# Value rows laid as stripes for two token tiles, and one shared pass over the whole value table for the other two

## The chip, the cores and the metric

The kernel runs on one core of one Trainium2 chip. The metric is the device time of one execution in microseconds (us); of several runs the median is given. All arithmetic is in float32. The engines are TensorE (PE; PEld is its weight load), VectorE (DVE), ScalarE (ACT), GpSimd (POOL, which here issues the indirect gathers) and SyncE (SP, which issues the plain transfers).

## What is computed

One transformer block on 512 tokens of width 1024. Attention (8 "forgetting" heads, 4 differential heads) comes first, then a retrieval layer (PEER): each token has 8 query heads, each head picks its 16 best of 128 x 128 = 16384 experts, and an expert is one row of `u_tab` and one row of `v_tab` (1024 float32, 4 KB each).

```python
q = (xb @ w_q).reshape(PEER_TOKEN_BLOCK, PEER_HEADS, 2, PEER_HALF_DIM)
sc = jnp.einsum('thpd,hpkd->thpk', q, sub_keys).astype(jnp.float32)
s1, i1 = lax.top_k(sc[:, :, 0], PEER_TOPK)
s2, i2 = lax.top_k(sc[:, :, 1], PEER_TOPK)
cand = (s1[..., :, None] + s2[..., None, :]).reshape(PEER_TOKEN_BLOCK, PEER_HEADS, -1)
...
top_s, pos = lax.top_k(cand, PEER_TOPK)
eidx = jnp.take_along_axis(cidx, pos, axis=-1)
g = jax.nn.softmax(top_s, axis=-1).astype(xb.dtype)
u_sel = jnp.take(u_tab, eidx, axis=0)
hid = jax.nn.gelu(jnp.einsum('thkd,td->thk', u_sel, xb), approximate=False) * g
v_sel = jnp.take(v_tab, eidx, axis=0)
return jnp.einsum('thk,thkd->td', hid, v_sel)
```

So each token has 128 picks (8 heads x 16), and each pick wants a dot product with a u row and a weighted addition of a v row. The block ends with an RMS norm.

## The kernel before

**Tiles and stages.** The 512 tokens are four tiles of 128, one token to a partition. Attention is done for tile 0 first, then for tiles 1, 2 and 3 together (GROUPS). An order written by a planner (`ORDER`, lists of pieces such as `project`, `attend`, `outproj`, `query`, `keys`) is followed by PE, ACT and DVE alike. From the moment tile 0's first head has its scores, the retrieval layer of tile 0 is hosted in the same program: its steps are laid between the pieces of tiles 1 to 3 (`pieces_in`). Then a loop over tiles 1, 2, 3 does their retrieval alone.

**The search** (`topk_first`, `topk_second`) finds one head's 16 experts on DVE, lines 1123 to 1193. In the loop its first half follows one group of four dots and its second half the next.

**u rows.** POOL gathers one pick of all 128 tokens with one indirect transfer (L507, 128 rows of 4 KB = 512 KB) into a ring of four. DVE multiplies it with `hn` and sums (L1208, `dot`); ACT makes the gelu of four at once (L903); DVE multiplies with the gate (L1218).

**v rows.** POOL gathers them the same way (L515) into another ring of four, with u and v transfers by turns. For tile 0, DVE adds each row times its coefficient to `h` (L1228). For tiles 1 to 3, ACT makes a diagonal matrix of the coefficients (L910) and PE multiplies it with the row, in two halves of 512 columns, adding up in two PSUM banks (L730). A tile thus costs 256 gathers, 134 MB.

**Weights** of the projections come as 48 loads of 1 MB on SP's queue (L465) in pieces of 1 KB. PE turns the sub-keys over itself (`subkeys`).

## Time and profile before

| | |
|---|---|
| median of 2 runs | 1873.81 us (1871.68 to 1875.94) |
| span of the profiled execution | 1856.5 us |
| PE, DVE, POOL busy | 72%, 65%, 62% of the span |
| moved by DMA | 594 MB, 320 GB/s over the span |
| of which indirect gathers | 537 MB in 1024 transfers |

The span runs from the first to the last instruction; the profiled execution's own time is thus 1856.5 us plus what lies around it. Busy shares are averages over stages with different limits, so the stretches are read one by one: 0 to 123 us (tile 0's attention up to its first search), 123 to 535 (until the last attention piece of tile 3), 535 to 687 (queries and keys of tiles 1 to 3, and the rest of tile 0's retrieval), and three stretches of 390 us, one for each tile of the loop. In a timeline row the columns are start, duration, engine, line, operation, out<-in, count, and in brackets the idle time before it and who ended it. One float32 matmul of the program shows as two records.

### The profile page before, as it was taken

The numbers are of one execution on the slowest core, as the hardware profiler recorded it, in microseconds if no ns is written. First come the engines' busy times: TensorE is split into PE (matmuls) and PEld (weight loads), VectorE is DVE, ScalarE is ACT, GpSimd is POOL, SyncE is SP. The second block draws the span as 40 slices with busy tenths as digits, with TensorE's granted clock in tenths as the row PEclk, the third lists the DMA queues.
The fourth block names the chain that finished last, engine by engine and source line by source line (L and its number), as shares of the span: only waits on it lengthen the run. The fifth ranks groups of instructions, "written<-read, shape, count | busy, mean of one in ns | idle before, by whom it ended". The sixth has DMA issues, their size and how long they took to land.

```text
span 1856.5 us, 16630 instructions
## 1 busy us (share of the span) xinstructions
PE 1343.4 (72%) x3547; PEld 631.9 (34%) x3547; DVE 1198.2 (65%) x2864; ACT 439.1 (24%) x1049; POOL 1145.1 (62%) x1034
## 2 busy tenths in 40 slices
PE   6976898985588857666666666766777677766776
PEld 5655465572245532222222222222222222222222
DVE  2237768888998766665665566565665666656564
ACT  2323123343332122122121122112121221212112
POOL 0005645663456647777777767777777677777774
PEclk9987987986698988999999999999999999999899
DMA  9449968996689969999999999999999999999997
GB/s 305 152 139 353 348 238 277 322 346 232 229 300 325 345 228 339 347 365 348 342 365 335 347 330 349 351 352 356 347 364 327 338 372 354 365 342 368 340 360 263
DMA packets 196531, 594.24 MB, mean 320 GB/s; under 512 B 18544, under 2 KB 59512, under 8 KB 196472
## 3 DMA queue, kind: packets, MB, share of 16 engines
q0 software_dynamic: 147456, 536.94, 79.0%
q1 hardware_dynamic: 49016, 56.67, 9.3%
q8 instruction: 19, 0.31, 0.1%
q14 instruction: 40, 0.33, 0.1%
HBM read 591.44 MB, written 2.10 MB: 320 GB/s over the span
## 4 chain that ended last, share of the span: by engine, by line
DMA 26%; issue 14%; PE 12%; DVE 10%; POOL 7%; ACT 1%; DVEq 0%; POOLq 0%
DMA v_ring<-in_peer_v_dram,eidx 15%; DMA u_ring<-in_peer_u_dram,eidx 11%; PE acc L730 6%; DVE u_ring L1208 4%; POOL u_ring L507 4%; PE mm L580 3%; POOL v_ring L515 3%; PE acc L580 1%; DVE onehot L1175 1%; DVE picked L1186 1%; DVE onehot L1182 0%; DVE top_p L1165 0%; DVE top_v L1155 0%; DVE top_v L1162 0%; DVE top_hl L1169 0%
## 5 line engine op out<-in xcount | busy, mean ns | idle before, releaser
L730 PE MATMUL acc<-v_ring,diag 128*128 128x512 f32 x1536 | 802.2, 650 | 366.4 <-DMA v_ring<-in_peer_v_dram,eidx 353.6
L1208 DVE CUSTOM_DVE_ANT_0 u_ring<-u_ring,hn 128x1024 f32<-128x1024 f32 x512 | 619.4, 1224 | 388.4 <-DMA u_ring<-in_peer_u_dram,eidx 386.8
L507 POOL DMA_INDIRECT u_ring<-in_peer_u_dram,eidx x512 | 565.8, 1105 | 471.1 <-DVE hid L1208 185.4
L515 POOL DMA_INDIRECT v_ring<-in_peer_v_dram,eidx x512 | 577.2, 1127 | 226.3 <-issue 118.2
L730 PEld LDWEIGHTS acc<-v_ring,diag 128*128 128x128 f32 x1536 | 278.5, 200 | 889.5 <-issue 790.1
L903 ACT ACTIVATE gel<-hid 128x4 f32<-128x4 f32 x128 | 26.2, 205 | 880.1 <-DVE hid L1208 879.9
L1228 DVE SCALAR_TENSOR_TENSOR h<-v_ring,coef,h 128x1024 f32<-128x1024 f32 x128 | 164.4, 1285 | 4.4 <-DMA v_ring<-in_peer_v_dram,eidx 1.0
L910 ACT ACTIVATE diag<-ident,coef 128x128 f32<-128x128 f32 x384 | 131.7, 393 | 91.8 <-PE acc L730 62.3
L580 PE MATMUL mm<-actT,w_ring 128*128 128x384 f32 x336 | 126.1, 534 | 15.9 <-DMA w_ring<-in_w_in_dram 6.3
L580 PEld LDWEIGHTS mm<-actT,w_ring 128*128 128x128 f32 x336 | 69.3, 211 | 67.7 <-issue 20.9
L572 PE MATMUL mm<-w_ring,actT 128*128 128x256 f32 x304 | 77.0, 412 | 1.9 <-issue 0.8
L572 PEld LDWEIGHTS mm<-w_ring,actT 128*128 128x128 f32 x304 | 62.4, 210 | 13.0 <-issue 1.8
L580 PE MATMUL acc<-actT,w_ring 128*128 128x384 f32 x176 | 62.6, 511 | 3.6 <-issue 3.6
L903 ACT ACT_TABLE_LOAD x49 | 62.9, 1283 | 0.9
L1218 DVE TENSOR_TENSOR coef<-gel,gate 128x4 f32<-128x4 f32 x128 | 20.6, 161 | 57.2 <-ACT gel L903 57.2
L887 ACT ACTIVATE s_maps<-s_maps,negmax 128x128 f32<-128x128 f32 (+3 forms) x64 | 35.7, 558 | 75.1 <-DVE negmax L1084 74.8
L707 PE MATMUL tr<-ident,s_maps 128*128 128x128 f32 x120 | 26.8, 329 | 36.0 <-ACT pT L895 35.3
L690 PE MATMUL sc<-store 64*128 64x384 f32 (+3 forms) x86 | 35.0, 531 | 18.0 <-DVE negmax L1084 16.1
L580 PEld LDWEIGHTS acc<-actT,w_ring 128*128 128x128 f32 x176 | 34.9, 202 | 28.6 <-issue 8.4
L1208 DVE DVE_READ_ACCUMULATOR2_ANT hid<- 128x1 f32 x512 | 42.0, 82 | 0.0
L640 PE MATMUL mm<-w_ring,store 128*128 128x512 f32 x80 | 41.4, 668 | 0.0
L719 PE MATMUL o<-v_all,pT 128*128 128x64 f32 (+1 forms) x240 | 39.0, 302 | 0.4 <-ACT pT L895 0.2
(192 smaller groups left out, 1055.2 us busy)
## 6 DMA issues: line engine op xcount, KB each, us to landing
w_ring<-in_w_in_dram SPq DMA_DIRECT2D x18, 1024.0 KB, 11.1
w_ring<-in_peer_w_q_dram SPq DMA_DIRECT2D x16, 1024.0 KB, 8.8
u_ring<-in_peer_u_dram,eidx POOLq DMA_INDIRECT x512, 6.1
v_ring<-in_peer_v_dram,eidx POOLq DMA_INDIRECT x512, 6.2
v_ring<-in_w_in_dram SPq DMA_DIRECT2D x6, 1024.0 KB, 12.3
w_ring<-in_w_out_dram SPq DMA_DIRECT2D x6, 1024.0 KB, 11.3
h<-in_x_dram SPq DMA_DIRECT2D x4, 512.0 KB, 6.5
v_ring<-in_w_out_dram SPq DMA_DIRECT2D x2, 1024.0 KB, 5.0
```

The costliest lines, as they stand in the source:

```text
L507: nc.gpsimd.indirect_dma_start(out=u_ring[:, c % U_RING, :], out_offset=None, in_=peer_u[0], in_offset=bass.IndirectOffsetOnAxis(ap=eidx[p ...
L515: nc.gpsimd.indirect_dma_start(out=v_ring[:, c % V_RING, :], out_offset=None, in_=peer_v[0], in_offset=bass.IndirectOffsetOnAxis(ap=eidx[p ...
L572: last = nc.tensor.matmul(bk[:, 0:SLAB], actT[:, c, j * P:(j + 1) * P], w[:, c, :], start=(c == 0), stop=(c == KC - 1))
L580: last = nc.tensor.matmul(bk[:, 0:n], w[:, c, q * P:(q + 1) * P], actT[:, c, 0:n], start=(c == 0), stop=(c == KC - 1))
L640: last = nc.tensor.matmul(bk[:, :], qT[:, KC // 2 * hf + c, j * P:(j + 1) * P], w[:, c, :], start=(c == 0), stop=(c == KC // 2 - 1))
L719: last = nc.tensor.matmul(o_b[:, col:col + w], pT[:, k % 2, q * P:(q + 1) * P], v_all[:, q, vcol:vcol + w], start=(q == 0), stop=(q == t))
L730: last = nc.tensor.matmul(acc[half][:, :], diag[:, c % COLS, :], v_ring[:, c % V_RING, half * BANK:(half + 1) * BANK], start=(starts and c ...
L887: nc.scalar.activation(s, s, ACT.Exp, scale=-1.0, bias=negmax[:, m:m + 1], accum_out=rowsum[:, m:m + 1]).then_inc(exp_done, 1)
L903: nc.scalar.activation(gel[:, par, g0:g0 + COLS], hid[:, par, g0:g0 + COLS], ACT.Gelu).then_inc(gelu_done, 1)
L910: nc.scalar.activation(diag[:, c, :], ident[:, :], ACT.Copy, scale=coef[:, par, g0 + c:g0 + c + 1]).then_inc(diag_done, 1)
L1208: nc.vector.tensor_tensor_reduce(out=u_ring[:, c % U_RING, :], in0=u_ring[:, c % U_RING, :], in1=hn[:, :], scale=1.0, scalar=0.0, op0=ALU. ...
L1228: nc.vector.scalar_tensor_tensor(out=ht, in0=v_ring[:, c % V_RING, :], scalar=coef[:, par, c:c + 1], in1=ht, op0=ALU.mult, op1=ALU.add).th ...
```

## The change

- **Gathers.** The two rings of four become one ring of five slots of 512 KB (`row_ring`, ROWS). POOL's order is: 128 u rows of tile 0, 128 v rows of tile 0, the 384 u rows of tiles 1 to 3, the 128 v rows of tile 3. There are 768 indirect transfers in place of 1024.
- **Stripes** (tiles 0 and 3). A v transfer now fetches all 128 picks of one token, one to a partition. The picks' numbers and coefficients are turned over on PE (`swap`), and PE multiplies the row block with a weight of 32 columns of which one holds the token's coefficients (`pads`, `fill_pad` on DVE, `stripes` on PE). Four tokens go to four groups of 32 PSUM partitions. A step `i` has four tokens, each with two products of 512 columns; the next step's pad waits until the last has been used.
- **Shared pass** (tiles 1 and 2). DVE makes one-hot matrices for four tokens at a time (`onehots`), ACT scales one of them (four copies of 128 columns), PE multiplies them (four products of 128 columns) and ACT keeps the 512 results as weights (`keep_weights`): 32 such groups for each tile, until `region_a` and `region_b` hold, for tile 1 and tile 2, the weight of each token for each of the 16384 experts. Then SP streams the value table once in 128 blocks of 512 KB, and PE multiplies each block with both tiles' weights, four products of 512 columns (`values`).
- **Search.** Two heads are searched by one run of instructions (`topk`), at double width where the data allow it.
- **Order.** Tile 0's v steps stand behind the last attention piece, among the queries of tiles 1 to 3. All of tile 1's dots stand behind tile 0's last stripe; tile 2's dots are woven with the 32 weight groups of tile 1; 32 of tile 3's dots with those of tile 2; the other 96 with the pass over the table; tile 3's stripes stand behind the pass and behind the closing norms of tiles 1 and 2.
- **Layouts.** The host lays out the slabs in pieces of 8 KB for a partition and the sub-keys already turned; PE's turns of them and of the first gain are gone. The slab ring has three places.

```diff
-U_RING = 4
-V_RING = 4
-            def gather_u(n, par, c):
-                if not (isinstance(n, int) and n == 0 and c < U_RING):
-                    pool.wait_ge(dot_done, TOPK * n + c + 1 - U_RING)
...
-            def gathers(n, par, last):
-                for c in range(TOPK):
-                    ahead = c + COLS
-                    if ahead < TOPK:
-                        gather_u(n, par, ahead)
-                    elif not last:
-                        if ahead == TOPK:
-                            numbers_of(n + 1)
-                        gather_u(n + 1, 1 - par, ahead - TOPK)
-                    gather_v(n, par, c)
+ROWS = 5
+V_SLOTS = 4
+TOKENS = 4
+COLS = 32
+STRIPES = 4
...
+    early += [(16.0 + 8.0 * s, ("dots", 0, s)) for s in range(QUARTERS)]
+    met = max(16.0 + 8.0 * QUARTERS, PACE * attended + 1)
+    early += [(met + 1, ("coef", 0)), (met + 2, ("swap", 0))]
+    early += [(met + 12 + 6.0 * i, ("stripes", 0, i)) for i in range(COLS)]
...
+    ORDER += [("coef", 1), ("spread", 1)]
+    for s in range(QUARTERS):
+        ORDER += [("dots", 2, s), ("weights", 1, s)]
+        if s in (2, 8):
+            ORDER += searches(2, (s + 10) // 6)
+        if s in (12, 16, 20, 24):
+            ORDER += searches(3, (s - 12) // 4)
+    ORDER += [("gexp", 3, PH // 2 - 1), ("weights_end", 1), ("coef", 2), ("spread", 2)]
+    for s in range(QUARTERS):
+        ORDER += [("weights", 2, s)] + ([("dots", 3, s // 4)] if s % 4 == 3 else [])
+    ORDER += [("weights_end", 2)]
+    done_dots, done_rows = QUARTERS // 4, 0
...
+    ORDER += [("drain", 1), ("scale", 1), ("drain", 2), ("scale", 2)]
+    ORDER += [("stripes", 3, i) for i in range(done_rows, COLS)] + [("drain", 3), ("scale", 3)]
...
+            def row_free(r):
+                if r < ROWS:
+                    return
+                which, t = ROW_RUNS[(r - ROWS) // P]
+                c = (r - ROWS) % P
+                if which == "u":
+                    pool.wait_ge(dot_done, P * t + c + 1)
+                else:
+                    pool.wait_ge(row_used, P * GATHERED.index(t) + c + 1)
+                pool.nop(nofuse=True)
+            gather_scores(0)
+            gather_values(0)
+            for t in range(1, TILES):
+                gather_scores(t)
+            gather_values(TILES - 1)
...
+            def stripes(t, i):
+                k = COLS * GATHERED.index(t) + i
+                pe.wait_ge(pad_done, k + 1)
+                for g in range(STRIPES):
+                    r = row_no("v", t, STRIPES * i + g)
+                    pe.wait_ge(row_in[r % ROWS], 16 * (r // ROWS + 1))
+                    for half in range(2):
+                        last = nc.tensor.matmul(acc[t][half][COLS * g:COLS * (g + 1), :],
+                                                pads[:, g, COLS - 1 - i:2 * COLS - 1 - i],
+                                                row_ring[:, r % ROWS, BANK * half:BANK * (half + 1)],
+                                                start=(i == 0), stop=(i == COLS - 1), skip_group_check=True)
+                    last.then_inc(row_used, 1)
+            def weights(t, g):
+                k = GROUPS_W * MIXED.index(t) + g
+                pe.wait_ge(onehot_done, k + 1)
+                pe.wait_ge(scaled, k + 1)
+                if k >= len(w_banks):
+                    pe.wait_ge(w_copied, k + 1 - len(w_banks))
+                for i in range(TOKENS):
+                    last = nc.tensor.matmul(w_banks[k % len(w_banks)][:, i * P:(i + 1) * P],
+                                            picks_c[:, k % 2, i, :], picks_a[:, k % 2, i, :], start=True, stop=True)
+                last.then_inc(w_full, 1)
+            def values(m):
+                if m == 0:
+                    pe.wait_ge(w_copied, len(MIXED) * GROUPS_W)
+                    pe.wait_ge(drained, 2)
+                pe.wait_ge(v_in[m % V_SLOTS], 16 * (m // V_SLOTS + 1))
+                for t in MIXED:
+                    for half in range(2):
+                        last = nc.tensor.matmul(acc[t][half][:, :], wts[t][:, m, :], v_slots[m % V_SLOTS][:, BANK * half:BANK * (half + 1)],
+                                                start=(m == 0), stop=(m == K1 - 1), skip_group_check=True)
+                last.then_inc(v_used, 1)
...
-            def add_row(n, par, c):
-                dve.wait_ge(v_in[c % V_RING], 16 * (TOPK // V_RING) * n + 16 * (c // V_RING + 1))
-                dve.wait_ge(coef_done, GRP * n + c // COLS + 1)
-                if n or c:
-                    dve.wait_ge(v_used, TOPK * n + c)
-                ht = h[:, n // PH, :]
-                nc.vector.scalar_tensor_tensor(out=ht, in0=v_ring[:, c % V_RING, :], scalar=coef[:, par, c:c + 1], in1=ht,
-                                               op0=ALU.mult, op1=ALU.add).then_inc(v_used, 1)
...
+                elif kind == "weights":
+                    t, g = p
+                    k = GROUPS_W * MIXED.index(t) + g
+                    act.wait_ge(onehot_done, k + 1)
+                    for i in range(TOKENS):
+                        one = picks_c[:, k % 2, i, :]
+                        at = 2 * P + TOKENS * g + i
+                        last = nc.scalar.activation(one, one, ACT.Copy, scale=tcols[:, at:at + 1])
+                    last.then_inc(scaled, 1)
+                    if g > 0:
+                        keep_weights(t, g - 1)
+            def keep_weights(t, g):
+                k = GROUPS_W * MIXED.index(t) + g
+                act.wait_ge(w_full, k + 1)
+                nc.scalar.activation(wts[t][:, :, g * TOKENS:(g + 1) * TOKENS],
+                                     w_banks[k % len(w_banks)][:, :].rearrange("p (t i) -> p i t", t=TOKENS),
+                                     ACT.Copy).then_inc(w_copied, 1)
+            def fill_pad(t, i):
+                k = COLS * GATHERED.index(t) + i
+                if k > 0:
+                    dve.wait_ge(row_used, STRIPES * k)
+                nc.vector.tensor_copy(pads[:, :, COLS - 1:COLS], tcols[:, i:P:COLS].unsqueeze(2)).then_inc(pad_done, 1)
+            def onehots(t, g):
+                k = GROUPS_W * MIXED.index(t) + g
+                if k >= 2:
+                    dve.wait_ge(w_full, k - 1)
+                lo = g * TOKENS
+                for kept, at in ((picks_a, lo), (picks_c, P + lo)):
+                    last = nc.vector.tensor_tensor(out=kept[:, k % 2, :, :], in0=iota_f[:, :].unsqueeze(1).broadcast_to([P, TOKENS, K1]),
+                                                   in1=tcols[:, at:at + TOKENS].unsqueeze(2).broadcast_to([P, TOKENS, K1]),
+                                                   op=ALU.is_equal)
+                last.then_inc(onehot_done, 1)
...
+            def load_values(m):
+                if m < 2:
+                    sp.wait_ge(mm_full, len(MM))
+                elif m < V_SLOTS:
+                    sp.wait_ge(w_full, len(MIXED) * GROUPS_W)
+                else:
+                    sp.wait_ge(v_used, m - V_SLOTS + 1)
+                sp.dma_start(v_slots[m % V_SLOTS], peer_v[0][m * P:(m + 1) * P, :]).then_inc(v_in[m % V_SLOTS], 16)
```

**Place 1: DVE, between the dots of a tile after tile 0.** L1208 (before) and L1235 (change) are the dot of one gathered u row. In the loop of before, four dots are followed by the first half of the search for one head:

```order
1125 L1208 ISA u_ring,hid<-u_ring,hn 128x1024
1126 L1208 ISA hid 128x1
1127 L1217 ISA
1128 L1218 TENSOR_TENSOR coef<-gel,gate 128x4
1129 L1123 ISA
1130 L1123 COPY tk_s<-store 128x256
1131 L1112 ISA
1132 L1127 MAX tk_v<-tk_s 128x8 x2
```

In the change, twelve to twenty-four dots stand in a row, and then the whole search for two heads (it goes on for 13 more rows):

```order
677 L1235 ISA row_ring,hid<-row_ring,hn 128x1024
678 L1235 ISA hid 128x1
679 L1171 MAX topk_mem<-region_b 128x8 x4
680 L1174 MATCH_REPLACE topk_mem<-topk_mem,region_b 128x128 x4
681 L1176 MAX_INDEX topk_mem<-topk_mem,region_b 128x8 x4
682 L1179 MAX topk_mem<-topk_mem 128x8 x4
683 L1182 MAX_INDEX topk_mem<-topk_mem 128x8 x4
684 L1183 TENSOR_TENSOR topk_mem<-topk_mem 128x512
685 L1187 CAST topk_mem<-topk_mem 128x64
686 L1191 MAX gate<-topk_mem 128x8 x2
```

The search has moved from small pieces between groups of four dots to one block in front of the next dots.

**Place 2: PE, the queries of tiles 1 to 3.** Before, L580 are the query products (384 columns for three tiles) and L665 the key scores, with nothing else between them:

```order
288 L580 MATMUL mm<-actT,w_ring 128x384 x16
289 L580 MATMUL acc<-actT,w_ring 128x384 x8
290 L665 MATMUL mm<-subkT,qyT 128x128 x4
291 L665 MATMUL acc<-subkT,qyT 128x128 x2
292 L580 MATMUL mm<-actT,w_ring 128x384 x16
293 L665 MATMUL acc<-subkT,qyT 128x128 x2
294 L665 MATMUL mm<-subkT,qyT 128x128 x4
295 L580 MATMUL acc<-actT,w_ring 128x384 x8
```

In the change, L590 and L673 are the same products, and L707 are the striped products of tile 0 (32 result columns of weight, 512 moving columns; eight are one step of four tokens):

```order
258 L590 MATMUL bank<-region_a 128x384 x8
259 L707 MATMUL bank<-row_ring,pads 32x512 x8
260 L590 MATMUL bank<-region_a 128x384 x8
261 L707 MATMUL bank<-row_ring,pads 32x512 x16
262 L590 MATMUL bank<-region_a 128x384 x8
263 L707 MATMUL bank<-row_ring,pads 32x512 x8
264 L673 MATMUL bank<-region_b,stream 128x128 x6
265 L590 MATMUL bank<-region_a 128x384 x8
266 L707 MATMUL bank<-row_ring,pads 32x512 x16
```

PE has taken over tile 0's v rows, which DVE added before, and they stand between the queries.

**Place 3: PE, the end of the program.** Before, the loop body ends with a product pair for each v row of the tile:

```order
462 L730 MATMUL acc<-v_ring,diag 128x512 x2
463 L728 REGISTER_ALU
464 L730 MATMUL acc<-v_ring,diag 128x512 x2
465 L728 REGISTER_ALU
466 L730 MATMUL acc<-v_ring,diag 128x512 x2
467 L749 REGISTER_ALU
468 L749 COMPARE_AND_BRANCH
```

In the change the last blocks of the value table (L731, with the weights of tile 1 in `region_a` and of tile 2 in `region_b`) are followed by all 256 striped products of tile 3:

```order
561 L731 MATMUL bank<-stream,region_b 128x512 x2
562 L731 MATMUL bank<-stream,region_a 128x512 x2
563 L731 MATMUL bank<-stream,region_b 128x512 x2
564 L731 MATMUL bank<-stream,region_a 128x512 x2
565 L731 MATMUL bank<-stream,region_b 128x512 x2
566 L707 MATMUL bank<-row_ring,pads 32x512 x256
567 L290 UNCONDITIONAL_BRANCH
```

The v rows of the last tile stand behind the whole pass, on PE and on DVE alike.

## Rows read from the trace of the kernel before

**Rows 1.** Stretches: start:end, length, busy us (records) by engine, PE clock, DMA, GB/s
```profile
core 0: us, PE busy (x) PEld busy (x) DVE busy (x) ACT busy (x) POOL busy (x), PEclk, DMA share, GB/s
0.00:123.00 123.00, 97.99 (x423) 73.05 (x423) 30.42 (x95) 35.10 (x102) 2.05 (x10) 0.93 0.61 197
123.00:535.00 412.00, 321.69 (x1180) 207.79 (x1180) 342.50 (x753) 134.88 (x284) 217.91 (x187) 0.83 0.82 288
535.00:687.00 152.00, 121.51 (x408) 72.55 (x408) 117.26 (x215) 36.34 (x78) 86.56 (x73) 0.90 0.88 319
687.00:1077.00 390.00, 256.29 (x500) 88.56 (x500) 235.63 (x601) 77.07 (x195) 285.38 (x256) 0.96 0.93 341
...
1467.00:1856.50 389.50, 274.00 (x519) 95.54 (x517) 236.18 (x602) 78.70 (x197) 270.99 (x252) 0.94 0.92 342
```

**Rows 2.** The page's chain that ended last, by engine
```profile
DMA 26%; issue 14%; PE 12%; DVE 10%; POOL 7%; ACT 1%; DVEq 0%; POOLq 0%
```

**Rows 3.** Groups by shape in the loop, 690 to 1856 us: count, busy, mean, idle before
```profile
L730 PE MATMUL acc<-v_ring,diag 128*128 128x512 f32 x1536 | 802.2, 650 | 366.4 <-DMA v_ring<-in_peer_v_dram,eidx 353.6 <-ACT diag L910 12.5
L1208 DVE CUSTOM_DVE_ANT_0 u_ring<-u_ring,hn 128x1024 f32<-128x1024 f32 x384 | 463.3, 1225 | 380.1 <-DMA u_ring<-in_peer_u_dram,eidx 379.4 <-DVE hn L1235 0.6
...
L1175 DVE TENSOR_TENSOR onehot<-top_hlf,iota_f 128x512 f32<-128x512 f32 x24 | 16.6, 692 | 2.5
```

**Rows 4.** Stretch 123 to 535 us, DVE's dots (L1208) alone
```profile
123.00:535.00 412.00, 112.89 (x184) 0.83 0.82 288
```

**Rows 5.** The same stretch, DVE's row additions (L1228) alone
```profile
123.00:535.00 412.00, 112.49 (x88) 0.83 0.82 288
```

**Rows 6.** Timeline of DVE, the first search of one head, first and last instruction
```profile
122.92 0.29 DVE L1123 COPY tk_s<-store 128x256 f32<-128x256 f32 x1 [12.66 <-ACT store L863]
...
131.84 0.15 DVE L1193 TENSOR_SCALAR gneg<-top_v 128x1 f32<-128x1 f32 x1
```

**Rows 7.** Timeline of DVE, dots that find their rows landed
```profile
1820.68 1.23 DVE L1208 CUSTOM_DVE_ANT_0 u_ring<-u_ring,hn 128x1024 f32<-128x1024 f32 x1
...
1821.83 1.22 DVE L1208 CUSTOM_DVE_ANT_0 u_ring<-u_ring,hn 128x1024 f32<-128x1024 f32 x1
```

**Rows 8.** Timeline of PE, dense products: 8 of 384 columns, then 4 of 512
```profile
206.63 5.32 PE L580 MATMUL acc<-actT,w_ring 128*128 128x384 f32 x16
...
548.29 3.60 PE L640 MATMUL acc<-w_ring,store 128*128 128x512 f32 x8
```

**Rows 9.** Timeline of PE, two score products on the two halves of its rows
```profile
50.46 0.37 PE L690 MATMUL sc<-store 64*128 64x128 f32 x1
50.47 0.37 PE L690 MATMUL acc<-store 64*128 64x128 f32 x1
```

**Rows 10.** Timeline of POOL and DVE, the first gathers and the first dot
```profile
132.86 1.09 POOL L507 DMA_INDIRECT u_ring<-in_peer_u_dram,eidx  x1 [130.05 <-DVE gsum L1200]
134.26 0.94 POOL L507 DMA_INDIRECT u_ring<-in_peer_u_dram,eidx  x1 [0.30 <-issue]
...
137.65 1.23 DVE L1208 CUSTOM_DVE_ANT_0 u_ring<-u_ring,hn 128x1024 f32<-128x1024 f32 x1 [4.69 <-DMA u_ring<-in_peer_u_dram,eidx]
```

**Rows 11.** The page's DMA issues: count, median us from issue to landing
```profile
u_ring<-in_peer_u_dram,eidx POOLq DMA_INDIRECT x512, 6.1
v_ring<-in_peer_v_dram,eidx POOLq DMA_INDIRECT x512, 6.2
```

**Rows 12.** Timeline of PE, one v row of the loop (two products)
```profile
1219.78 1.98 PE L730 MATMUL acc<-v_ring,diag 128*128 128x512 f32 x4 [1.30 <-DMA v_ring<-in_peer_v_dram,eidx]
```

**Rows 13.** Timeline of ACT, four scaled copies of 128 columns
```profile
1205.77 1.28 ACT L910 ACTIVATE diag<-ident,coef 128x128 f32<-128x128 f32 x4 [0.31 <-DVE coef L1218]
```

**Rows 14.** Groups by shape up to 660 us, ACT's copies of 512 columns from PSUM
```profile
L895 ACT ACTIVATE pT<-tr 128x512 f32<-128x512 f32 x12 | 7.0, 583 | 2.2 <-PE tr L707 2.1
```

**Rows 15.** Timeline of the last tile's closing norm and store
```profile
1848.90 1.29 DVE L1247 TENSOR_TENSOR fin<-acc,h 128x512 f32<-128x512 f32 x2 [8.62 <-PE acc L730]
...
1853.48 0.33 SPq L486 DMA_DIRECT2D out_dram<-fin  x1
```

936 lines of the change are left out of this document (457 added, 479 removed).

## The prediction

> **What bounds the kernel now.** I read the stretches first [rows 1]. In the loop a tile takes 390 us, DMA is busy 92 to 93% at 341 to 342 GB/s, and no engine is above 73%. The groups of the loop say the same from the other side: PE waits 354 of its 366 idle us for v rows, DVE 379 of 380 for u rows [rows 3], and DMA leads the chain [rows 2]. So the loop is bound by its gathers: 390 us for 256 rows, 1.52 us a row, and search, diagonals and products all lie beside them. Before the loop it is different. From 123 to 535 us DVE is busy 343 of 412 us and PE 322, at 288 GB/s [rows 1]: two engines that wait for each other at close quarters. The profiled span is 1856.5 us and the median 1873.8, so 17.3 us lie around the span; I add them at the end.
>
> The change takes 67 MB out of 594 (two tiles' 134 MB of v rows against one table of 67 MB). At the loop's rate that is some 195 us. The question is whether transfers stay the bound. The new order puts the work in a row instead of side by side, so I cost it stage by stage, by what ends last in each.
>
> **A, start to first search: 125 us** (123 before). The turns of the sub-keys are gone and slabs come in larger pieces (minus 8), but the first search now wants head 1's keys too (plus 10).
>
> **B, tile 0's dots beside attention, 123 to 535 before: 380 us.** DVE loses 88 row additions, 112 us [rows 5], and gains the 36 of 128 dots that it has not done by then (184 records are 92 dots [rows 4]; one dot takes 1.15 us, start to start [rows 7]), 41 us. Its seven searches (9.1 us each, from 122.92 to 131.99 [rows 6]) become four of a pair. I cost a pair at 15.5 us: twice 9.1 less the copy and the small steps that are done once for both (bounds 14 and 18). DVE falls to about 275 us, and no longer sets the stage; PE's 322 us stay, with their waits for ACT and DVE. Bounds 322 and 412. The dots and searches come in its first half, where DVE is still the busier one, so I stay near the upper: 380.
>
> **C, queries of tiles 1 to 3 with tile 0's stripes: 250 us.** The stretch 535 to 687 (152 us) had 121.5 us of PE work [rows 1]; with the last output products it is 132. New are 256 products of 512 columns. Four such take 3.60 us with the drain, 0.855 us each [rows 8]; a step of eight is 6.8 us one after another, 219 in all. But two products on different halves of the array start 0.01 us apart [rows 9], so I expect the four 32-column groups to run beside each other, near 1.7 us a step, 55 in all. PE then needs 187 us; serial it would be 351. The rows set the rest: one v row occupies its slot from issue to landing (6.1 us [rows 11]), for PE's 1.98 us [rows 12] and the 0.3 us until POOL moves [rows 10], 8.4 us; with five slots that is 1.68 us a row, 215 for 128. And PE is away for 5.3 us with each of 16 query products [rows 8] while the ring stands full, of which I count some 35 us as not hidden. 250, bounds 187 and 351. Before, all of this and more lay in 152 us since the rows had been spread over B.
>
> The Trainium skill (TensorE: Matmul & The Clock Gate, Part 3) says that matmuls of 32 columns whose outputs lie in different groups of 32 partitions run at the same time, and gives 2.38 times for three of them. By that the striped step would be about 2.9 us, an estimate from the page's factor and the 6.8 us; the row of two halves starting together agrees in kind. The sum would be the same, the serial rival would fall.
>
> **D, tile 1's dots alone: 282 us.** Nothing else runs. A u row's slot is taken 6.1 + 1.15 + 0.3 = 7.55 us, a fifth is 1.51 us, the same as the loop's 1.52: 128 rows are 192 us. Now the searches stand in the way: six pair searches (four of tile 1, two of tile 2) of 15.5 us, 93 us, in which only the five slots fill. That gives back 1.5 us each, minus 9; the first gather behind the first search adds 6. Before, the same searches were hidden under the gathers, since DVE had 380 us to spare. Bounds: 246 (dots at 1.15) and 300.
>
> **E, tile 2's dots with tile 1's weight groups: 288 us.** A quarter of four dots (4.6) plus two one-hots of 512 elements (0.65 to 0.69 each [rows 3]) is 5.9 us of DVE, as much as four rows need; 32 of them 189, six searches 93, the turn between tiles 6. ACT's part of a group is 1.28 us for four scaled copies [rows 13] and some 0.6 to 0.8 for the 512-column copy [rows 14], hidden here. Bounds 280 and 305.
>
> **F, tile 2's weight groups with 32 dots: 90 us.** ACT needs 2.1 us a group, 67; DVE 32 x 1.3 + 32 x 1.15 = 78 and hands over at each; with turn and last copies 90. Bounds 76 and 105.
>
> **G, the pass: 439 us.** 128 blocks of four products, 512 x 0.855 = 438. This is the dearest term. The dense rows show no way out: 8 products of 384 columns take 5.32 us and 4 of 512 take 3.60, each with a drain of some 0.18, the same 1.67 ns for a column [rows 8], with weight loads hidden. Table and 96 u rows are 117 MB, 270 GB/s, well under the loop's 341: the transfers wait for PE here. Bounds 437 and 445.
>
> **H, tile 3's stripes alone: 228 us.** DVE first closes tiles 1 and 2 (4.6 us from drain to store [rows 15], 5.5 with ACT's squares, twice 11), then 5 of 128 rows are there (2 us), 123 come at 1.68 us (207), then the last norm and store, 8. Bounds: 178 (rows at POOL's 1.24 us from issue to issue [rows 10]) and 264 (stripes serial, 7.4 us a step).
>
> **Sum.** 125 + 380 + 250 + 282 + 288 + 90 + 439 + 228 = 2082 us of span, 2099 with the 17.3. The loop's 1169 us become 1327 (D to H), and the part before it, 687, becomes 755. 67 MB fewer are moved, but 438 us of PE products, 93 + 93 us of searches and the last tile's 207 us of rows no longer lie beside one another. What loses the cover: in G the gathers of tile 3's v rows could have run (only five do), in D and H PE stands still, in D and E DVE's searches are bare.
>
> **Rivals.**
> - *Transfers stay the bound.* If POOL, SP and the engines ran ahead of each other far enough, what follows tile 0 would be bytes: 335 MB (five times 67) at 342 GB/s, 981 us, after 687: 1685 with the 17.3. For it speaks that this is how the loop works today. Against it: a ring of five slots cannot run ahead by more than 7.5 us, and the pass alone costs 438 us of PE for 117 MB. It decides if D to H come to less than 1130 us (0.04).
> - *Every stage at its floor*: 118 + 322 + 187 + 246 + 280 + 76 + 437 + 178 = 1844, 1861 with the rest: no change (0.02).
> - *Faster rows.* With few transfers in flight a gather may land sooner than 6.1 us; then POOL's 1.24 us sets the pace. C falls by 35, D by 30, H by 50: 1984 (0.08). For it: the first gather of all, issued at 132.86, is in use at 137.65, 4.8 us later [rows 10]. Against it: 512 KB in 1.24 us is 423 GB/s, and the stretches of [rows 1] show no more than 342. The Trainium skill (DMA: Bandwidth & Descriptors, on the SWDGE path) gives about 2.0 us plus bytes over 436 GB/s for such a transfer, 3.2 us for 512 KB as an estimate; the trace's 6.1 is nearly twice that, and by the page's figure H would be at POOL's pace.
> - *Stripes run one after another*: C 351, H 254, 2226 (0.12). For it: each token's two halves share a column group and stand in a row, and nothing in the trace shows column groups.
>
> **Numbers.** The forecast's case has 0.74, its own range is 2040 to 2160 (B, C and H by 30 each). The range for 8 in 10 reaches to the serial stripes and leaves out the faster rows and the two cases below: 1990 to 2226. About 2% is what a measurement of this kernel can tell from no change. Faster by over 2%: 0.04; within: 0.02; slower: 0.94.
>
> **What would show it.** PE busy near 440 us without a gap in the pass, DMA near 270 GB/s there; DVE in D busy all through with idle gaps only between dots, 15 to 16 us for a pair search with POOL waiting meanwhile; POOL's idle time ended by dots and by striped products; PE nearly idle in D and H; in H about 1.7 us a row; the four striped products of a step starting close together. I would be wrong if the pass took much under 430 us, if the rows' pace left 1.5 to 1.7 us, or if C hid the stripes under the queries altogether.

## The result and the profile after the change

The changed kernel takes 2248.3 us (median of two runs, 2247.4 to 2249.2) where the kernel before, measured beside it, takes 1873.8: a ratio on record of 1.196 [1.187, 1.204] (the two medians alone give 1.200). That is slower, as forecast, but 149 us above the forecast 2099 and 22 us outside the range. The profiled run took 2247.4 us for a span of 2245.5, so only 1.9 us lie around the span, not the 17.3 that I had added: by spans the sum was 2082 and missed 163 us.

The stretches of the changed kernel, at the borders of the forecast's stages A to H (columns as in [rows 1]; a border can be drawn 1 or 2 us to either side):

```profile
core 0: us, PE busy (x) PEld busy (x) DVE busy (x) ACT busy (x) POOL busy (x), PEclk, DMA share, GB/s
0.00:129.00 129.00, 102.70 (x428) 76.79 (x429) 29.38 (x93) 33.82 (x101) 2.15 (x10) 0.91 0.55 200
129.00:433.00 304.00, 202.27 (x718) 131.94 (x718) 234.08 (x551) 50.87 (x132) 159.85 (x128) 0.79 0.78 273
433.00:557.00 124.00, 106.27 (x432) 67.50 (x432) 48.30 (x138) 43.67 (x101) 0.00 (x0) 0.88 0.12 43
557.00:855.00 298.00, 264.05 (x934) 103.66 (x933) 14.34 (x45) 27.76 (x58) 120.52 (x128) 0.96 0.74 254
855.00:1153.00 298.00, 0.95 (x4) 0.50 (x3) 241.04 (x615) 5.05 (x22) 167.84 (x133) 0.51 0.67 232
1153.00:1461.00 308.00, 65.47 (x256) 56.98 (x256) 273.09 (x671) 63.43 (x191) 163.40 (x128) 0.50 0.66 220
1461.00:1562.00 101.00, 55.36 (x259) 50.55 (x259) 78.61 (x133) 56.05 (x161) 36.71 (x30) 0.67 0.46 151
1562.00:2004.00 442.00, 441.47 (x1026) 195.34 (x1026) 122.25 (x203) 4.99 (x9) 143.55 (x99) 1.00 0.72 270
2004.00:2245.50 241.50, 199.28 (x513) 44.40 (x512) 15.22 (x47) 6.17 (x16) 115.55 (x123) 0.96 0.79 274
```

| stage | forecast | measured | missed |
|---|---|---|---|
| A start | 125 | 129 | +4 |
| B tile 0's dots beside attention (two rows above) | 380 | 428 | +48 |
| C tile 0's stripes beside the queries | 250 | 298 | +48 |
| D tile 1's dots | 282 | 298 | +16 |
| E tile 2's dots, tile 1's weights | 288 | 308 | +20 |
| F tile 2's weights, 32 dots | 90 | 101 | +11 |
| G pass | 439 | 442 | +3 |
| H tile 3's stripes, closing | 228 | 241 | +13 |

Against [rows 1] one sees where the loop's overlap went. No stage moves 341 GB/s on average any more. PE is busy for 441 of the pass's 442 us at full clock, at 270 GB/s, as forecast. D has PE at nothing, H has DVE at next to nothing. The pass's average hides two halves, which the forecast had not told apart, with tile 3's dots beside it and without them:

```profile
1562.00:1762.00 200.00, 199.47 (x461) 88.34 (x462) 119.61 (x196) 3.55 (x8) 138.84 (x94) 0.99 1.02 402
1762.00:2004.00 242.00, 242.00 (x567) 107.00 (x565) 2.63 (x8) 1.44 (x2) 4.70 (x5) 1.00 0.48 160
```

The first moves 402 GB/s, more than any stage before the change, so 341 GB/s was not a ceiling for all transfers; the second moves 160, with POOL doing five gathers in 242 us. The chain of work that ended last is led by PE now, where DMA led it [rows 2], and the page's groups show the costs of a row:

```profile
PE 45%; DVE 22%; DMA 16%; issue 11%; POOL 4%; ACT 2%; POOLq 0%; DVEq 0%; ACTq 0%
...
L537 POOL DMA_INDIRECT row_ring<-in_peer_u_dram,eidx x512 | 666.6, 1302 | 664.8 <-DVE hid L1235 362.2
L1235 DVE CUSTOM_DVE_ANT_0 row_ring<-row_ring,hn 128x1024 f32<-128x1024 f32 x512 | 618.0, 1225 | 217.9 <-DMA row_ring<-in_peer_u_dram,eidx 215.0
L548 POOL DMA_INDIRECT row_ring<-in_peer_v_dram,row_t x256 | 240.8, 941 | 657.1 <-PE bank L707 410.5
L707 PE MATMUL bank<-row_ring,pads 128*32 128x512 f32 x1024 | 345.2, 628 | 66.8 <-DMA row_ring<-in_peer_v_dram,row_t 33.3
```

POOL stands 362 us for dots (L1235) and 410 us for striped products (L707): the five slots are what the gathers wait for. 200 of the 410 are one wait, from 1819 us to the first striped products of H: tile 3's first five v rows fill the ring, and nothing uses them before the pass is over. And a u row's gather takes POOL 1302 ns where a v row's takes 941, with the same instruction.

### The profile page after: what moved, and what is told of

Its sections match the earlier page's. It is cut to its first block, busy times and chain, and to the rows that moved or that the text cites. A ratio compares the mean times of both kernels' runs of the same rounds, so it can differ in the third digit from the quotient of the medians.

```text
span 2245.5 us, 14698 instructions
## 1 busy us (share of the span) xinstructions
PE 1437.8 (64%) x4564; PEld 727.7 (32%) x4564; DVE 1056.3 (47%) x2494; ACT 291.8 (13%) x788; POOL 909.6 (41%) x778
## 4 chain that ended last, share of the span: by engine, by line
PE 45%; DVE 22%; DMA 16%; issue 11%; POOL 4%; ACT 2%; POOLq 0%; DVEq 0%; ACTq 0%
PE bank L731 20%; DMA row_ring<-in_peer_u_dram,eidx 10%; PE bank L707 9%; DVE row_ring L1235 7%; DMA row_ring<-in_peer_v_dram,row_t 6%; PE bank L590 4%; PE bank L582 4%; POOL row_ring L537 4%; PE bank L647 3%; DVE stream L1283 2%; PE bank L720 2%; PE bank L785 1%; DVE topk_mem L1209 1%; DVE topk_mem L1214 1%; DVE topk_mem L1217 1%
## 5 line engine op out<-in xcount | busy, mean ns | idle before, releaser
L537 POOL DMA_INDIRECT row_ring<-in_peer_u_dram,eidx x512 | 666.6, 1302 | 664.8 <-DVE hid L1235 362.2
L1235 DVE CUSTOM_DVE_ANT_0 row_ring<-row_ring,hn 128x1024 f32<-128x1024 f32 x512 | 618.0, 1225 | 217.9 <-DMA row_ring<-in_peer_u_dram,eidx 215.0
L548 POOL DMA_INDIRECT row_ring<-in_peer_v_dram,row_t x256 | 240.8, 941 | 657.1 <-PE bank L707 410.5
L707 PE MATMUL bank<-row_ring,pads 128*32 128x512 f32 x1024 | 345.2, 628 | 66.8 <-DMA row_ring<-in_peer_v_dram,row_t 33.3
L720 PE MATMUL bank<-stream 128*128 128x128 f32 x512 | 120.0, 416 | 285.5 <-issue 235.7
L731 PE MATMUL bank<-stream,region_a 128*128 128x512 f32 x512 | 242.5, 596 | 0.7 <-ACT region_b L973 0.7
L731 PE MATMUL bank<-stream,region_b 128*128 128x512 f32 x512 | 240.6, 592 | 0.0
L707 PEld LDWEIGHTS bank<-row_ring,pads 128*32 128x32 f32 x1024 | 78.7, 112 | 322.0 <-issue 138.6
L590 PE MATMUL bank<-region_a 128*128 128x384 f32 x512 | 180.7, 511 | 1.5 <-issue 0.8
L582 PE MATMUL bank<-region_a 128*128 128x256 f32 x512 | 129.7, 413 | 14.6 <-DVE stream L1033 13.0
L731 PEld LDWEIGHTS bank<-stream,region_a 128*128 128x128 f32 x512 | 97.6, 191 | 123.0 <-issue 122.0
L731 PEld LDWEIGHTS bank<-stream,region_b 128*128 128x128 f32 x512 | 97.5, 190 | 123.0 <-issue 123.0
L590 PEld LDWEIGHTS bank<-region_a 128*128 128x128 f32 x512 | 100.3, 200 | 78.8 <-issue 20.5
L582 PEld LDWEIGHTS bank<-region_a 128*128 128x128 f32 x512 | 105.0, 210 | 32.7 <-issue 15.7
## 6 DMA issues: line engine op xcount, KB each, us to landing
region_b<-in_keys_t_dram SPq DMA_DIRECT2D x1, 1024.0 KB, 12.6
```

Source lines behind the costliest of these rows:

```text
L537: nc.gpsimd.indirect_dma_start(out=row_ring[:, r % ROWS, :], out_offset=None, in_=peer_u[0], in_offset=bass.IndirectOffsetOnAxis(ap=eidx[: ...
L548: nc.gpsimd.indirect_dma_start(out=row_ring[:, r % ROWS, :], out_offset=None, in_=peer_v[0], in_offset=bass.IndirectOffsetOnAxis(ap=row_t[ ...
L582: last = nc.tensor.matmul(bk[:, 0:SLAB], actT[:, c, j * P:(j + 1) * P], w[:, c, :], start=(c == 0), stop=(c == KC - 1))
L590: last = nc.tensor.matmul(bk[:, 0:n], w[:, c, q * P:(q + 1) * P], actT[:, c, 0:n], start=(c == 0), stop=(c == KC - 1))
L707: last = nc.tensor.matmul(acc[t][half][COLS * g:COLS * (g + 1), :], pads[:, g, COLS - 1 - i:2 * COLS - 1 - i], row_ring[:, r % ROWS, BANK ...
L720: last = nc.tensor.matmul(w_banks[k % len(w_banks)][:, i * P:(i + 1) * P], picks_c[:, k % 2, i, :], picks_a[:, k % 2, i, :], start=True, s ...
```

## The experiments

All are edits of the changed kernel. The kernel before, measured again beside each group of them, came out at medians of 1853 to 1879 us, up to 1.4% apart; so sizes below are read from stretches of the traces, and medians only where they differ by more. The changed kernel itself was not measured again beside them. rows4, bareB, nostripes0, onehalf and thin6 are single runs. The tables give lengths in us.

### The ring's depth: rows4, rows6

`ROWS = 5` becomes 4 and 6 (for room, rows6 gives the value table three slots and loads one of its blocks early, not two).

> The changed kernel with a ring of four rows instead of five. Theory 'a slot's time sets the pace': in the changed kernel a u row comes every 1.61 us in the stretch of tile 1's dots and a v row every 1.75 us in tile 3's stripes, five slots, so a slot is taken 8.05 and 8.75 us; with four it is 2.0 and 2.2 us a row: tile 1's dots 298 -> about 345 us, the last stretch (tile 3's stripes and closing) 241 -> about 295, tile 0's stripes 298 -> about 345, in all about 2420 to 2450. Rival 'POOL's issue sets the pace of u rows (1.26 us of gather and 0.3 between), PE's serial products (4 x 0.43 us) that of v rows': tile 1's dots stay near 300 unless four slots take over at 6.1+1.15+0.3 = 7.55 us, 1.89 a row (+25 us at most), the last stretch stays within 15 us; in all under 2350.

> The changed kernel with a ring of six rows; for the room the value table's slots are three instead of four and only the first block is loaded early. Theory 'a slot's time sets the pace': 1.34 us for a u row, 1.46 for a v row, tile 1's dots 298 -> about 270, the last stretch 241 -> about 205, tile 0's stripes 298 -> about 270, in all about 2140 to 2160. Rival 'POOL's issue and PE's serial products set the pace': tile 1's dots 298 and the last stretch 241 unchanged, 2240 to 2255. The pass stays at 442 us in both (a block's slot is free for 3 x 3.45 us).

Measured: 2383.5 and 2169.2 us (ratio 1.167 [1.159, 1.174]).

| slots | B | C | D | H | 24 rows between two searches of D | v row in H |
|---|---|---|---|---|---|---|
| 4 | 454 | 324 | 330 | 274 | 44.9 | 2.06 |
| 5 | 428 | 298 | 298 | 241 | 38.5 | 1.81 |
| 6 | 408 | 280 | 289 | 217 | 38.0 | 1.63 |

(The v row's pace is first product to last in H, over the rows that come after the ring's first filling. C runs from the swap to the last striped product.) Each theory holds in a part. In C and H, where PE uses the rows, and in B, where DVE has attention to do beside them, the gain goes on with the sixth slot. In D it all but stops at five: 38.5 and 38.0 us for the same 24 rows. (The pass, expected to stay at 442 us, took 451 in rows6; the total is so much the higher.) And a slot's time isn't fixed as I had assumed: H's pace times the slots is 8.2, 9.1 and 9.8 us, so with more slots each is taken for longer.

### What slows a u row: thin6

rows6 with dots over 64 of the 1024 columns:

```
-                    nc.vector.tensor_tensor_reduce(out=row_ring[:, r % ROWS, :], in0=row_ring[:, r % ROWS, :], in1=hn[:, :],
+                    nc.vector.tensor_tensor_reduce(out=row_ring[:, r % ROWS, 0:64], in0=row_ring[:, r % ROWS, 0:64], in1=hn[:, 0:64],
```

> rows6 with dots over 64 of the 1024 columns (the rest of each dot is left out): DVE is nearly idle between rows, all rows are still gathered whole. Theory 'DVE at work slows POOL's gather issue from 0.94 to 1.3 us, which with 0.3 between sets 1.58 us a row': the issue falls to 0.94 us and a u row to 1.24 to 1.3 us in the stretch of tile 1's dots (24 rows between two searches in 30 to 31 us instead of 38). Rival 'the transfers set it': 1.5 to 1.6 us a row still.

POOL from the end of D's second search to the start of its third, in the changed kernel, in rows6, in thin6 and in rows4 (count, busy us, mean ns, idle before):

```profile
L537 POOL DMA_INDIRECT row_ring<-in_peer_u_dram,eidx x23 | 30.7, 1336 | 20.2 <-DVE hid L1235 13.5 <-issue 6.7
```
```profile
L537 POOL DMA_INDIRECT row_ring<-in_peer_u_dram,eidx x22 | 30.6, 1391 | 20.0 <-DVE hid L1235 13.5 <-issue 6.4
```
```profile
L537 POOL DMA_INDIRECT row_ring<-in_peer_u_dram,eidx x23 | 21.5, 937 | 20.1 <-DVE hid L1235 13.5 <-issue 6.6
```
```profile
L537 POOL DMA_INDIRECT row_ring<-in_peer_u_dram,eidx x23 | 30.8, 1340 | 26.6 <-DVE hid L1235 21.7 <-issue 4.9
```

In thin6 the issue falls to 937 ns, the 24 rows from 38.0 to 29.1 us, D by 40 us to about 249; the whole takes 2036.6 us. The 13.5 us of waiting for a dot are the search before the stretch. With five and six slots POOL waits for nothing more, so between searches it is POOL's own issue that paces u rows (1.3 to 1.4 us and 0.3 between); with four it waits 8 us more, and the slots count as well. The issue is long because DVE's dots run: behind pieces of searches in early's C, 79 gathers take 991 ns each. The Trainium skill names the sharing: the GPSIMD Engine Reference (Specifications, row on the SBUF interfaces) has GpSimd's access to SBUF contend with DVE instructions with two SBUF inputs, which the dots are; 937 against 1391 ns fits that. The row gives no size and does not speak of gathers.

### The searches: split, early

split cuts every search of D and E but the first in pieces, one behind each group of four dots:

```
-        if s in (2, 8, 14):
-            ORDER += searches(1, (s + 4) // 6)
...
+        if s >= 2:
+            ORDER += pieces(*((1, (s + 4) // 6) if s < 20 else (2, (s - 20) // 6)), (s - 2) % 6, 6)
```

> The changed kernel with each pair search from tile 1's second on cut in pieces of seven to eight steps, one behind each group of four dots, instead of 13.7 us at one stretch. Theory 'rows and searches stand one after another, as the ring holds five rows only': DVE's small gaps between dots (1.61 - 1.18 us a row) take the pieces in; tile 1's dots fall from 298 to about 245 us (DVE alone: 128 x 1.18 + 6 x 13.7 = 233), tile 2's from 308 to about 285 (DVE alone 273), in all about 2170 to 2190. Rival 'DVE and POOL slow each other, so that a row takes 1.6 us of gather issue whenever DVE works': each piece just makes the gathers late, the gain is under 30 us: 2220 to 2250.

Measured: 2178.1 us (1.175 [1.168, 1.183]); D 272, E 278. E fell 7 us below its forecast (DVE 271 of 278 us busy: it is DVE's stretch). D stayed 27 above its own. There the issue still takes 1262 ns, and POOL still waits 39 us for dots; the two were not told apart. early takes the pieces out of D and E instead, three behind each striped step of tile 0 from the thirteenth on:

```
+    for i, p in enumerate(tail):
+        ORDER.append(p)
+        if p[0] == "stripes":
...
+            take(3)
```

> The changed kernel with the searches of tiles 1 to 3 in six pieces each, three pieces behind each striped step of tile 0 from its thirteenth on, where DVE has nothing but pads; only six searches' worth of pieces less one stay in tile 1's dots. Theory 'D and E are long since 12 searches stand bare in them': both become 128 rows at 1.6 us, 205 to 225 us instead of 298 and 308; C stays near 298 (pieces of 7 us lie beside a step of 8.9 us), in all 2248 - 165 = about 2080. Rival 'pieces hold up the pads, and C grows by what D and E lose': 2180 or more.

```profile
546.00:852.00 306.00, 263.09 (x934) 102.00 (x934) 150.07 (x627) 33.65 (x98) 129.13 (x133) 0.98 0.75 255
852.00:1078.00 226.00, 0.87 (x3) 0.50 (x3) 184.67 (x381) 3.08 (x12) 155.57 (x128) 0.50 0.86 294
1078.00:1303.00 225.00, 66.35 (x259) 57.49 (x259) 194.63 (x329) 56.56 (x161) 148.51 (x128) 0.50 0.88 303
```

These are C, D and E of early. Ten of the twelve searches are in C now; the other two lie in pieces in D. DVE does 136 us more in C and C grows by 8; D and E lose 155, a little more than the ten searches' 138 us. The whole takes 2086.6 us (1.126 [1.119, 1.133]), forecast 2080. The prediction had called the searches of D and E bare, and they are, by their full size.

### Tile 0's dots beside attention: bareB, spreadB

bareB puts all of them behind the attention, spreadB a group of four every 13.6 shares instead of every 8:

```
-    early += [(16.0 + 8.0 * s, ("dots", 0, s)) for s in range(QUARTERS)]
+    early += [(16.0 + 13.6 * s, ("dots", 0, s)) for s in range(QUARTERS)]
```

> The changed kernel with all of tile 0's searches and dots moved behind the attention of tiles 1 to 3. It shows what the attention needs alone. Theory 'tile 0's dots and searches hold DVE, and with it attention, in the first 304 us (to 433), while rows, POOL and PE have room': attention alone goes at the pace that it has after 433 (120 us for 41% of the order's shares, 0.63 us a share), 461 shares in 290 us, so the last tile's mix is at about 420 us instead of 552. Rival 'attention is slow by itself (PE, ACT and DVE hand over at every map)': the last mix is still at 500 or later. Behind it the dots (4 searches of 13.7 us and 128 rows of 1.6 us, less what the ring holds) and then tile 0's stripes stand bare, about 2280 in all by the theory, over 2350 by the rival.

> The changed kernel with tile 0's dots and searches spread over the whole attention (a group of four dots every 13.6 shares instead of every 8). Theory 'DVE bounds the first 304 us and is idle in the 124 behind them': the stretch from the first search to the swap falls from 428 to 370 to 390 us, in all 2190 to 2215. Rival 'every share of attention costs what it costs and the dots are filled in at no matter which place': 428 stays, 2240 to 2255.

bareB's attention alone, and spreadB's stage B:

```profile
129.00:434.00 305.00, 278.80 (x1123) 183.67 (x1122) 71.58 (x191) 84.38 (x207) 0.00 (x0) 0.93 0.18 62
```
```profile
122.00:508.00 386.00, 303.21 (x1152) 198.74 (x1151) 280.12 (x691) 91.80 (x231) 152.47 (x128) 0.85 0.65 229
```

The last mix begins at 433.8 us in bareB and at 551.8 in the changed kernel: from the first search of the latter on, attention alone takes 305 us, not 423. Spread evenly the dots cost it 75 more instead of 118 (its last mix is at 502), B is 386 and the kernel 2206.4 us (1.189 [1.182, 1.197]). So 42 of B's 48 us come from the place of the dots: 254 of their 256 records lie before 433 us, where DVE is busy 234 of 304 us and holds the attention back, and in the 124 us behind them DVE has 48, POOL none and DMA 12%. With six slots and the old order B is 408, so slots take off a part of the same excess. bareB as a whole came to 2401 us, where the theory had 2280, and so on the side of its rival's "over 2350", though the last mix, which was to tell the two apart, is with the theory (420 against 500). The dots behind the attention take 273 us, and C stayed 294, since the swap waits for the dots and the queries stand behind it on PE, a wait that I had overlooked.

### Tile 0's stripes beside the queries: nostripes0, onehalf, seven

nostripes0 leaves out the gathers and products of tile 0's v rows, onehalf half of all striped products (`for half in range(1)`), and seven keeps everything but gives v rows more slots:

```
+        room = list(range(ROWS)) + ([] if which == "u" else list(range(ROWS, ROWS + 7)) if t == 0 else [ROWS + 7, ROWS + 8])
+        k = min(room, key=lambda k: last_in.get(k, -1 if k < ROWS else -1))
```

> The changed kernel without the gathers of tile 0's v rows and without its striped products (that part of tile 0's result is left out). It shows what the queries of tiles 1 to 3 need alone in the stretch that was 298 us. Forecast's theory: 132 us of PE work, about 150 us as before the change; 298 is then 128 rows at 1.75 us (224) plus some 75 us in which rows and queries stood in each other's way. Rival 'the queries themselves got longer (other slabs, other waits)': over 180 us alone. In all 2248 - 145 = about 2100, or over 2130.

> The changed kernel without the striped products of the second half of the value columns, for tiles 0 and 3 (that half of their result is left out): four of the eight products of a step. Theory 'striped products stand one after another, row by row as the rows land (0.86 us for each product, 1.72 a row), and beside the queries that makes PE the bound': PE's time for tile 0's steps falls from 146 to about 75 us and the stretch from swap to drain from 298 to 225 to 240; the last stretch, where only the slot is shortened by 0.86 us, falls from 241 by 128 x 0.86 / 5 = 22. Rival 'the ring bounds both stretches': both fall by 22 and no more.

> The changed kernel with more slots for value rows only: tile 0's get seven beside the five, in memory that attention has left, tile 3's two more. Theory 'the ring bounds C: a full ring waits whenever PE is at a query, and PE takes each row alone since it lands alone': C falls from 298 to PE's need, 122 us and 32 steps of 1.9 to 3 us, 185 to 220 us; tile 3's rows come at 8.7 / 7 = 1.25 us, the last stretch falls from 241 to 180 to 190. In all 2248 - 150 = about 2100, 2070 to 2120. Rival 'PE bounds C, as its 89% of busy time says': C stays over 270; in all 2170 or more.

nostripes0 takes 2013.8 us, 234.5 less. From swap to the first search of tile 1 it needs 62 us, where the theory had 150 for the queries alone: the rest of them (66 us of PE) lies beside D, where PE has room, and D takes 302, 4 more. So it is the stripes, standing between the queries, that keep the last of these out of D, and C costs 236 us more with them than without. onehalf takes 2206.6 us. seven takes 2149.0 (1.144 [1.136, 1.152]). C of onehalf, C of seven and H of seven:

```profile
552.00:833.00 281.00, 219.91 (x677) 84.09 (x675) 14.28 (x45) 27.69 (x58) 121.08 (x128) 0.89 0.77 269
```
```profile
550.00:799.00 249.00, 200.76 (x934) 91.82 (x934) 14.31 (x46) 27.32 (x58) 121.36 (x128) 0.92 0.83 304
1948.00:2150.00 202.00, 162.71 (x512) 40.90 (x512) 14.96 (x47) 6.17 (x16) 113.33 (x121) 0.96 0.87 322
```

Leaving out half the products takes 17 us off C and 17 off H, the same in both, as the ring's rival says (it had 22); PE's busy time in C falls by 44 us (264 to 220) and was not the bound. More slots with all products take off 49 and 38. The mechanism stands in the changed kernel's timeline (start, us, engine, line, count, idle before and its releaser):

```profile
614.99 5.43 PE L590 MATMUL bank<-region_a 128*128 128x384 f32 x16 [0.69 <-ACT region_a L879]
...
616.23 0.94 POOL L548 DMA_INDIRECT row_ring<-in_peer_v_dram,row_t  x1 [0.30 <-issue]
...
620.34 2.21 PE L707 MATMUL bank<-row_ring,pads 128*32 128x512 f32 x16
...
622.48 5.43 PE L590 MATMUL bank<-region_a 128*128 128x384 f32 x16
...
623.02 0.94 POOL L548 DMA_INDIRECT row_ring<-in_peer_v_dram,row_t  x1 [5.84 <-PE bank L707]
...
627.84 4.84 PE L707 MATMUL bank<-row_ring,pads 128*32 128x512 f32 x16
...
635.58 1.88 PE L707 MATMUL bank<-row_ring,pads 128*32 128x512 f32 x4 [2.90 <-DMA row_ring<-in_peer_v_dram,row_t]
```

While PE is at a query (L590, 5.43 us) the ring fills and POOL stands 5.84 us; the rows that it then asks for are late for PE at 635. And the four column groups do run side by side: a whole step of 16 records takes 2.21 us at 620.34, when its four rows have landed, and one row's four records take 1.88 at 635.58, when they come one by one. A row alone costs PE nearly as much as four together. That is why PE was busy 146 us with tile 0's stripes where I had 55. seven's C did not reach the 185 to 220 forecast: 249, at 304 GB/s, with the slabs of the queries in the same transfers; what keeps it 30 us above that was not tried. Its v rows in H, with seven slots, come every 1.52 us, which is the loop's rate before the change [rows 1].

### Tile 3's stripes in the pass: v3pass

```
+        if done_dots == QUARTERS:
+            since += 1
+            if since % 2 == 0 and done_rows < COLS:
+                ORDER += [("stripes", 3, done_rows)]
+                done_rows += 1
```

> The changed kernel with 28 of tile 3's 32 striped steps inside the pass, one behind every second block of the value table once tile 3's dots are done, and 4 behind it: most of the order 'all striped steps of tile 3 behind the pass' undone. Theory 'the four column groups run side by side when their rows are there, as at 2014.9 to 2018.6 us of the changed kernel, where a step begins with four products 15 ns apart': a step adds 1.7 to 3 us of PE, the pass is 500 to 530 us (transfers: 184 MB at 342 GB/s are 538 at most), the rest 50; pass and what follows 683 -> 550 to 580, in all about 2110 to 2140. Rival 'a step costs PE 6.8 us wherever it stands': the pass grows by 190, the rest falls by 195, in all 2235 to 2255.

2153.7 us (1.164 [1.157, 1.170]); pass 549.5, what follows 47.6, together 597 instead of 683. Its second part, from the last dot on, and PE's timeline in it:

```profile
1806.00:2106.00 300.00, 290.75 (x884) 104.31 (x887) 5.43 (x30) 0.00 (x0) 105.82 (x113) 1.00 0.83 292
```
```profile
1913.04 1.88 PE L725 MATMUL bank<-stream,region_b 128*128 128x512 f32 x4
1914.85 1.94 PE L701 MATMUL bank<-row_ring,pads 128*32 128x512 f32 x16
```

A step whose rows are there costs the pass 1.94 us (1914.85); on average PE is at one for 3.4 us (95 for 28). That is between the theory's 1.7 to 3 and the rival's 6.8, nearer the theory, and total and pass came 14 and 20 us above its bounds.

### Tile 0's stripes beside the later dots: late0, late0b, combo5, combo6, combo6b

late0 moves tile 0's steps behind every second group of dots in D and E; late0b fills the pad ahead of two groups and lets v and u rows alternate in the ring.

```
late0:
+        ORDER += [("dots", 1, s)] + ([("stripes", 0, 0 + s // 2)] if s % 2 else [])
...
late0b:
+        ORDER += ([] if s % 2 else [("stripes", 0, s // 2)]) + [("dots", 1, s)]
```

> The changed kernel with tile 0's striped steps moved from the queries into the stretches of tile 1's and tile 2's dots (one step behind every second group of four dots, its rows in the ring in that order), tile 0's coefficients kept apart until then. Theory 'C cost 298 us because the v rows stood in it, and PE, DVE and the ring each have room in D and E': from the swap to tile 1's first search 62 us as without the stripes, D and E each take 192 rows at 1.6 us plus six searches of which some 7 us each are bare: about 350 us each; in all 2248 - 236 + 95 = about 2110. Rival 'the v rows cost the same wherever they stand (1.75 to 2.2 us each)': D and E grow by 128 x 1.75 = 224 us, in all 2230 to 2250.

> late0 again, but each step's pad is filled ahead of the two groups of dots beside it and its four v rows alternate with the eight u rows in the ring. Theory 'late0 lost 308 us in the two stretches of dots since a step's four v rows stood in the ring until DVE had come to its pad, and DVE then had no u rows': with pads ahead each stretch is 192 rows at 1.6 us and about 45 us of bare searches, 350 instead of 444 and 470; in all 2316 - 210 = about 2105, 2150 at most. Rival 'v and u rows in one ring of five wait for each other wherever the pads are': 2280 or more.

2316.0 (1.250 [1.244, 1.256]) and 2326.3 us (1.255 [1.247, 1.262]): both theories of mine fell, and late0b's rival (2280 or more) came true. The stretch from swap to tile 1's first search did come to 62 us, but D and E took 446 and 471 in late0, and 463 and about 455 in late0b. Waits between 700 and 1000 us in late0, then in late0b (us in total, times, longest):

```profile
PEld bank L696 <- DVE pads L1264: 207.9, 11, 29.2
...
DVE row_ring L1224 <- DMA row_ring<-in_peer_u_dram,eidx: 125.7, 69, 8.1
...
PE bank L696 <- DMA row_ring<-in_peer_v_dram,row_t: 41.4, 5, 14.8
```
```profile
PE bank L704 <- DMA row_ring<-in_peer_v_dram,row_t: 157.9, 41, 13.7
DVE row_ring L1232 <- DMA row_ring<-in_peer_u_dram,eidx: 129.0, 70, 4.3
...
PEld bank L704 <- DVE pads L1272: 49.8, 8, 7.1
```

The waits for pads went, as meant (208 to 50 us), PE's waits for v rows took their place (41 to 158), and DVE's for u rows stayed (126 and 129). I read this as one first-in, first-out ring of five that passes every stop of either engine on to the other, a search of 13.7 us above all. But late0b's PE clock is 0.70 there, and eight records of products of v rows, begun at 708.35 us, take 5.48 us. How much of the loss is that slower hold and how much the ring was not told apart.

The next three put several edits together. They counted on late0's gain, or late0b's, and fell with it.

> late0, v3pass and split (searches in pieces between dots) together, five rows in the ring. If the three gains add: 2248 - 140 - 125 - 70 = about 1915; DVE's and the rows' floors in D and E (384 rows at 1.57 us, 603 us) leave 1900. Rival 'the rows take all that the pieces give back': D and E stay at 2 x 350, 1980.

> The same with six rows in the ring and three slots for the value table. Theory 'POOL's gather issue (1.26 us and 0.3 between) and not the slots sets the pace while DVE works': D and E as in combo5, less by 10 at most, the first part 20 us less and the end 5 less: about 1880. Rival 'slots still count where PE holds rows of a step': 40 to 60 us less than combo5.

> late0b, spreadB, v3pass, split and six rows in the ring together. From combo6 (2039): late0b's gain there up to 100 (its two stretches of dots 355 and 393 -> 300 and 320), spreadB 30: about 1910. Rival 'rows in the ring wait for the other engine still': 1990 or more.

2130.2, 2038.9 and 2034.1 us (ratios 1.150, 1.101 and 1.097, each within 0.009). combo5 misses 1915 by 215, and late0 alone had missed its number by 206. Six slots (combo6) gave 91 us there, more than the 79 in the plain kernel and far more than the 35 that the theory had: the shared ring was short of slots. combo6b took 5 us off combo6 where 130 were forecast. spreadB is in it and brings its gain (the swap begins at 506 us, not 541), but from the swap to the pass it needs 951 us where combo6 needs 925: alternating the rows cost 26 us.

### Causes together: best, best2

best is early, spreadB, v3pass and rows6 in one, with all 32 of tile 3's steps in the pass; best2 has seven's slots as well.

```
-            if since % 2 == 0 and done_rows < COLS:
+            if since % 7 in (2, 4, 6, 0) and done_rows < COLS:
```

> early with dots and searches of tile 0 spread over the attention (-42), six rows in the ring (-79, of which 24 lay in the stretches that early shortens: -55), tile 3's striped steps in the pass, now all 32 (-94 and some 15 more). If these add to early's 2080: about 1875, with 1845 to 1900 as the bounds, the same as the kernel before (1853) within 2%. Rival 'the gains overlap, since rows, PE and DVE now bound all stretches at once': 1930 or more.

> best with the same slots on top of its six. By the slot theory tile 0's steps beside the queries fall from 283 to 215 us, and in the second part of the pass, where a striped step costs PE 3.6 us (308 us for 56 blocks of 3.45 and 32 steps), a step falls towards 1.9, 308 -> 260; 1894 - 68 - 45 = about 1780, at most 1815: faster than the kernel before by 2 to 4%. Rival 'PE and the transfers bound both by now' (PE is busy 245 of 283 us and 297 of 308 there): 1870 or more.

best came to 1893.8 us, 1.021 [1.016, 1.026] of the kernel before (1854.5): within its forecast, and too near 2% to be told from no change. best2 came to 1824.6 against 1879.3, 0.970 [0.965, 0.974]: faster than both kernels, and 10 us above its forecast's upper bound of 1815. best2's stages C, D, E and the two parts of the pass:

```profile
503.00:758.00 255.00, 193.06 (x933) 87.97 (x932) 146.65 (x623) 32.48 (x94) 132.55 (x134) 0.92 0.84 304
758.00:968.00 210.00, 0.87 (x3) 0.50 (x3) 184.91 (x384) 3.67 (x14) 156.60 (x128) 0.50 0.90 315
968.00:1184.00 216.00, 66.37 (x259) 57.51 (x259) 193.70 (x329) 56.56 (x161) 158.82 (x129) 0.50 0.90 319
1283.00:1541.00 258.00, 253.64 (x579) 108.18 (x580) 121.18 (x202) 4.56 (x9) 134.78 (x93) 0.99 0.88 340
1541.00:1809.00 268.00, 265.91 (x943) 99.62 (x942) 5.89 (x34) 0.00 (x0) 119.91 (x128) 1.00 0.96 359
```

The pass's second part now has PE and DMA both full (266 of 268 us, 0.96 and 359 GB/s), D and E move 315 to 319 GB/s. The step from best to best2 was 69 us by the medians, 44 short of the forecast, and the traces agree: C went 283 to 255 where 215 was expected (as in seven), the pass's second part 308 to 268 where 260 was. (Against the kernel before, which was 1.3% slower beside best2, the step is larger, 1.021 to 0.970.)

## Why the prediction was right and where it was wrong

**Right**: the side, and its reason, a sum of times that no longer lie beside each other. The pass is 442 us of PE at full clock without a gap (439 forecast); *transfers stay the bound* (1685) and *all floors* were ruled out. The searches of D and E stand bare (early: with ten of them moved under C, D and E fall by 155). PE is idle in D, DVE in H; closing takes 11 us before tile 3's stripes as said. Of my signs of being wrong one came true: the rows' pace left 1.5 to 1.7 us, with 1.81 in H and 2.32 in C. All eight stages missed to the same side, so the total's miss is their sum, 163 us of span.

**B, 380 for 428.** The step that failed is "DVE falls to about 275 us, and no longer sets the stage". DVE's busy time was nearly right (282 us; my terms add up to 270), but I set it against the whole stage, though the text says itself that dots and searches lie in its first half; the order puts them within 59% of attention's shares. There DVE holds the attention back (234 of 304 us busy), and in the rest it has 48 us of work in 124. With dots spread evenly the stage takes 386, within 6 of the forecast (spreadB).

**C, 250 for 298.** Two terms were short. "Some 35 us as not hidden" for PE's absences at 16 queries was short by 27: C's rows come every 2.32 us, H's every 1.81, over 123 rows 62 us (more slots give back 49). And 1.68 us a row from a fixed slot of 8.4 us was short by 16: H shows 1.81, 9.1 us a slot, over 123 rows, in C and again in H, whose whole miss is 13. The last 4 or 5 of C's 48 us lie at its start, 12.6 us from the swap to the first product. The 55 us for striped products were wrong too (146, since a row alone costs nearly what four together do), but by onehalf that cost the stage nothing beyond the slot. What I had not seen at all is that the queries need no full stretch of their own: without the stripes more than half of their PE work lies under D (nostripes0).

**D, 282 for 298.** The searches were cheaper (13.7 us for 15.5, minus 11 in six), the rows dearer by 27: the step that failed is "a fifth is 1.51 us, the same as the loop's 1.52", a slot's time shared by five with POOL's issue left out. At four slots the slots do bind in part; at five the issue beside dots, 1.34 us and 0.3 between, is slower than a fifth of a slot (thin6). The 1.24 us issue to issue of [rows 10] were read where DVE was idle. The loop before could have told: its 256 gathers a tile, 1.10 us each and 0.3 between, fill 358 of the 390 us, as much as DMA's 93%, while I had counted only POOL's busy share and called no engine above 73%; which of the two bounds the loop no run tells. **E** (+20) and **F** (+11) have the same rows and DVE's work; they were not taken apart further. E falls by 30 with split and by 15 with a sixth slot, so both causes of D reach into it.

**The serial stripes** (2226) came closest in number, by luck: products of a landed step do run side by side, and the rival's C of 351 us is 53 above the measured one. (Its H of 254 us and my bound of 264 for the same case disagree by 10.) *Faster rows* (1984) had POOL's 1.24 us right only for an idle DVE. D's first gather, issued at 870.92 us with no other under way, is used by the dot at 875.42, 4.5 us later. The Trainium skill's figure (DMA: Bandwidth & Descriptors, SWDGE path) gives 3.2 us for it, as an estimate. By that figure a slot of H would be taken 5.5 us, a fifth of it less than POOL's 1.24, and a sixth slot would have changed nothing there, an estimate too; it took 24 us off.

**The 17.3 us around the span** were 1.9 in the profiled run of the changed kernel: a difference between one profiled execution and a median of others is not a constant to be carried over.

## What to carry to other kernels

Cost a stage by where its work stands in the order, not by busy sums over the stage: a helper packed into the first 60% of its cover gets next to nothing from the rest. A short first-in, first-out ring between a gather and an in-order engine can add that engine's other work to the stage, whatever its share of busy time; ask for how long the consumer can be away, and compare it with the slots times the pace. Before a transfer scheme is swapped for one of fewer bytes, look for the small work (here searches) that had been free under it, and find it a new cover first.

## What the runs showed of the hardware that I had not expected

- POOL's issue of a gather takes 937 ns with DVE nearly idle, 991 behind pieces of searches (early's C) and 1336 to 1391 ns while DVE does dots of two 128x1024 operands.
- Plain and indirect transfers together move 402 GB/s over 200 us (pass, first half), where the loop before moved 341 with indirect ones alone.
- Striped products of 32 columns in four column groups run at the same time once their rows are there (16 records in 1.94 to 2.21 us, four of one row in 1.88). The Trainium skill (TensorE: Matmul & The Clock Gate, Part 3) says so, and these rows agree.
- Pace times slots in the gathers of v rows grows with the ring: 8.2, 9.1, 9.8 and (seven) 10.7 us with 4, 5, 6 and 7 slots.
- The granted clock is 0.50 to 0.51 in D and E, where PE does 1 and 65 us of work, the lower of its two levels (1.2 GHz), and 1.00 in the pass, the upper.
